# Compression products of a hybrid decoder layer, from full fp32 matmuls to three rounded products each

## What is computed

```
idx = CMP_STRIDE * jnp.arange(n_cmp)[:, None] + jnp.arange(CMP_LEN)[None, :]   # stride 16, length 32
def phi(rows, pe, w1, w2):
    blk = rows[:, idx] + pe[None, None, :, None, :]
    flat = jnp.moveaxis(blk, 3, 2).reshape(b, n_cmp, g, CMP_LEN * hd)
    return jax.nn.silu(flat @ w1) @ w2
kc, vc = rope(phi(k_raw, ...)), phi(v_raw, ...)
```

## Time and profile before

| | us |
|---|---|
| median of 3 runs (985.79 to 986.5) | 986.15 |
| the profiled execution | 986.04 |
| its span, first to last instruction | 984.1 |
| PE busy / DVE / ACT / POOL | 951.6 / 603.8 / 427.8 / 186.7 |

### The profile page before, as it was taken

The page is one execution under the profiler, slowest core; times in us unless marked ns, Lnnn a source line. Parts: engine busy times, 40 slices in busy tenths (PEclk is TensorE's granted clock), DMA queues, the critical chain, the costliest instruction groups (busy, mean ns, idle before and its releaser), DMA issues. The chain is left out here.

```text
span 984.1 us, 21068 instructions
## 1 busy us (share of the span) xinstructions
PE 951.6 (97%) x7852; PEld 865.2 (88%) x7852; DVE 603.8 (61%) x1377; ACT 427.8 (43%) x845; POOL 186.7 (19%) x320
## 2 busy tenths in 40 slices
PE   6999999999998999999999999999999989999996
PEld 6999888998776699999999999899877857999996
DVE  6998666675223467657679976766622225775564
ACT  6444655553220444344444465464521214443343
POOL 1100000337347500000000000003653644000000
PEclk9999999999999999999999999999999989999998
DMA  9673954736669763334546677553675878334421
GB/s 344 237 267 147 394 223 185 289 134 216 213 195 286 235 273 147 138 129 160 198 187 234 274 287 302 214 210 144 215 237 162 250 221 271 159 130 167 175 87 49
DMA packets 65477, 206.30 MB, mean 210 GB/s; under 512 B 12112, under 2 KB 49680, under 8 KB 56032
## 3 DMA queue, kind: packets, MB, share of 16 engines
q1 hardware_dynamic: 56480, 185.31, 51.2%
q0 software_dynamic: 8752, 19.63, 6.6%
q10 hardware_dynamic: 144, 0.01, 0.0%
HBM read 200.12 MB, written 40.18 MB: 244 GB/s over the span
## 5 line engine op out<-in xcount | busy, mean ns | idle before, releaser
L1641 DVE TENSOR_TENSOR big_r<-big,paged_r 128x1024 fp32r<-128x1024 f32 x160 | 195.0, 1223 | 86.5 <-ACT paged_r L1425 84.8
L971 PE MATMUL bank<-xnT_high_r,paged_r 128*128 128x288 f32 x768 | 231.7, 302 | 0.0
L971 PE MATMUL bank<-xnT_r,paged_r 128*128 128x288 f32 x704 | 207.7, 295 | 0.0
L971 PE MATMUL bank<-xnT_high_r,big_r 128*128 128x288 f32 x704 | 207.0, 294 | 0.0
L971 PE MATMUL bank<-short_r,big_r 128*128 128x288 f32 x576 | 170.4, 296 | 0.0
L1425 ACT ACTIVATE paged_r<-big 128x1024 fp32r<-128x1024 f32 x160 | 167.0, 1051 | 6.3 <-DMA big<-in_w_feat 4.0
L971 PEld LDWEIGHTS bank<-xnT_high_r,paged_r 128*128 128x128 f32 x768 | 144.1, 188 | 7.0 <-issue 5.3
L971 PE MATMUL bank<-short_r,paged_r 128*128 128x288 f32 x448 | 134.0, 299 | 9.6 <-DVE big_r L1641 9.4
L971 PE MATMUL bank<-kvp_r,paged_r 128*128 128x288 f32 x448 | 133.4, 298 | 0.0
L971 PEld LDWEIGHTS bank<-xnT_high_r,big_r 128*128 128x128 f32 x704 | 132.5, 188 | 0.0
L971 PEld LDWEIGHTS bank<-xnT_r,paged_r 128*128 128x128 f32 x704 | 132.3, 188 | 0.0
(11 more groups left out here) (317 smaller groups left out, 1466.4 us busy)
## 6 DMA issues: line engine op xcount, KB each, us to landing
big<-in_w_tok SPq DMA_DIRECT2D x13, 2048.0 KB, 8.9
big<-in_w_feat SPq DMA_DIRECT2D x12, 2048.0 KB, 8.4
big<-in_w_gate SPq DMA_DIRECT2D x10, 2048.0 KB, 8.6
out_kept_dil<-in_cache_dil SPq DMA_DIRECT2D x16, 1020.0 KB, 13.6
paged<-in_pool SPq DMA_DIRECT2D x218, 64.0 KB, 2.7
big<-in_w_up SPq DMA_DIRECT2D x12, 1024.0 KB, 9.2
paged<-in_pool POOLq DMA_DIRECT2D x166, 64.0 KB, 2.8
big<-in_kv_win SPq DMA_DIRECT2D x4, 2048.0 KB, 9.3
```

The source lines that it names most:

```text
L971: last = mm(out, l, r, start=(c == 0 and i == 0), stop=(c == n - 1 and i == 2))
L1641: v.tensor_tensor(l_part, full, h_part.bitcast(FP32), ALU.subtract).then_inc(*split_done.inc(s))
```

## The change

Seven things change. (1) A `hid` step is now a piece (hb, kind, bp, lh): one half of the page columns (`bp`), one half of the 8 rows of a column (`lh`), and both parts of w1. It is 4 x 2 x 3 = 24 products of fp32r with 128x128 weights and 256 columns, 16 pieces per layer. (2) ACT rounds the pages of a piece (`pround`, 1024 columns) into one of two buffers, DVE subtracts in place (`psplit`). This is written two pieces ahead: `begin()` stands behind every piece. (3) w1 is rounded and split alike in four quarters per layer (`wround`, `wsplit`), two of them in the units before, two between the first pieces. (4) The rounded w1 of the keys lies in the place of the residual `x`. So `x` is written to HBM by POOL at the start of layer 1 and is loaded again by SP in each layer ahead of the weights of `("gate", 0, 2)`. (5) Pages are loaded, waited for and freed by halves. (6) Both parts of a block now end in one bank after two pieces, and DVE makes one copy, one sum and one product of 256 columns (`hid` with lh = 1), once per `bp`, with a tanh of 256 columns on ACT. (7) `sscore 1 win` moves ahead of the piece 14, and the two `slc` scores of half 0 stand behind it, directly before the last piece (before: behind the 14th step, two steps from the end).

```diff
+    pieces = [(hb, kind, bp, lh) for hb in range(HB) for kind in range(2) for bp in range(2) for lh in range(2)]
+    begun = iter(pieces)
+    begin = lambda: [(kind,) + z for z in itertools.islice(begun, 1) for kind in ("pround", "psplit")]
+    w1_split = lambda kind, part: [("wround", kind, part), ("wsplit", kind, part)]
     blocks = {(0, 1): [("gates",)], (10, 0): [("ghid",)],
               (11, 0): [("ghidt",)], (12, 0): [("gkc",)], (13, 0): [("cscore", 0)], (14, 0): [("cturn", 0)],
-              (14, 1): [("cpv", 0), ("gateC", 0)], (15, 0): [("cscore", 1)]}
+              (12, 1): w1_split(0, 0), (13, 1): w1_split(0, 1),
+              (14, 1): [("cpv", 0), ("gateC", 0)], (15, 0): [("cscore", 1)] + begin(), (15, 1): begin()}
...
-           [("kc", 1)] + part(1, 1, 1, 1) + [("sgateA", 1), ("sscore", 0, "slc0"), ("sscore", 0, "slc1")] + \
-           part(1, 1, 0, 0) + [("sscore", 1, "cmp"), ("sexp", 1, "cmp"), ("sexp", 0, "slc")] + part(1, 1, 0, 1)
-    out += [("sscore", 1, "win"), ("cmpt", 1), ("sturn", 0, "cnew"), ("sscore", 1, "new"), ("sturn", 0, "slc0"), ("imp", 1),
+    done = iter(pieces)
+    piece = lambda: [("hid",) + next(done)] + begin()
+    out += [("sscore", 0, "d4"), ("pv", units[-2])] + piece() + w1_split(1, 0) + \
+           [("sscore", 0, "mix"), ("cturn", 1), ("pturn", units[-1], 0)] + piece() + \
+           [("sexp", 0, "A"), ("cpv", 1), ("pv", units[-1]), ("gateC", 1)] + w1_split(1, 1) + \
+           [("sscore", 0, "win"), ("sscore", 0, "new")] + piece() + \
+           [("sturn", 0, "d4")] + piece() + \
+           [("spv", 0, "d4"), ("sturn", 0, "mix"), ("sexp", 0, "win")] + piece() + \
+           [("spv", 0, "mix"), ("sturn", 0, "anew"), ("kc", 0)] + piece() + \
+           [("spv", 0, "anew"), ("soA", 0)] + piece() + \
+           [("sscore", 0, "cmp"), ("sexp", 0, "cmp"), ("sgateA", 0), ("sscore", 1, "d4")] + piece() + \
+           [("cmpt", 0), ("sscore", 1, "mix"), ("sturn", 0, "win"), ("sexp", 1, "A")] + piece() + \
+           [("vc", 0), ("spv", 0, "win"), ("sturn", 1, "d4")] + piece() + \
+           [("spv", 1, "d4"), ("sturn", 1, "mix"), ("imp", 0)] + piece() + \
+           [("impsum", 0), ("spv", 1, "mix"), ("sturn", 1, "anew")] + piece() + \
+           [("spv", 1, "anew"), ("soA", 1)] + piece() + [("kc", 1)] + piece() + \
+           [("sgateA", 1), ("sscore", 1, "win")] + piece() + \
+           [("sscore", 1, "cmp"), ("sexp", 1, "cmp"), ("sscore", 0, "slc0"), ("sscore", 0, "slc1"), ("sexp", 0, "slc")] + piece()
+    out += [("cmpt", 1), ("sturn", 0, "cnew"), ("sscore", 1, "new"), ("sturn", 0, "slc0"), ("imp", 1),
             ("spv", 0, "cnew"), ("vc", 1), ("sturn", 0, "slc1"), ("sexp", 1, "win"), ("impsum", 1)] + \
            splits(("gate", 0, 0), 0) + \
...
+    x_w, kvp_w = rounded("x", [P, 2048], "_w1"), rounded("kvp", [P, 4608], "_w1")
+    w1_low = rounded("long", [P, 4096], "_w1")
+    W1_HIGH = [[x_w[:, 0:1024], x_w[:, 1024:2048]], [kvp_w[:, 1536:2560], kvp_w[:, 2816:3840]]]
...
+    def page_parts(piece):
+
+        hb, kind, bp, lh = piece
+        slot = PAGE_SLOTS[("cmp", kind, hb)]
+        low = paged_r[slot][:, 2048 * bp:2048 * (bp + 1)].rearrange("p (m l g i) -> p g l m i", m=16, l=8, g=KV)
+        high = page_high[PIECES.index(piece) % 2].rearrange("p (m l g i) -> p g l m i", m=16, l=4, g=KV)
+        return [z.rearrange("p g l m i -> p g m l i") for z in (high, low[:, :, 4 * lh:4 * lh + 4, :, :])]
+
+    def piece_rows(z, piece):
+
+        _, _, bp, lh = piece
+        rows = z[:, 2048 * bp:2048 * (bp + 1)].rearrange("p (m n) -> p m n", m=16)
+        return rows[:, :, 64 * lh:64 * (lh + 1)]
+
+    def piece_high(piece):
+
+        return page_high[PIECES.index(piece) % 2].rearrange("p (m n) -> p m n", m=16)
...
+    def load_pages(queue, key, z, numbers):
+
+        kind, which, hb, h = key
+        if kind == "cmp" and hb == 0:
+            queue.wait_ge(*big_used(Now.layer, split_keys[which - 2]))
+        elif key[0:3] == ("slc", 0, 1):
             queue.wait_ge(*big_used(Now.layer, ("kA", 1)))
-        elif key == ("slc", 1, 1):
-            queue.wait_ge(*pages_used(Now.layer, ("cmp", requests[0] // 2, 1)))
...
         else:
             queue.wait_ge(*pages_used(*PG[z].before(key)))
         for i in page_share(key, z):
             b, g = divmod(i, PAGES)
-            if b in requests:
-                src = a["pool"][Now.layer, bass.ds(numbers[hb][i], 1), :, which + 2 * (kind == "slc"), :]
-                queue.dma_start(pgb(key)[:, b, g, :], src.rearrange("a p n -> (a p) n")).then_inc(*PG[z].fill(key))
...
-                        sp.wait_ge(*pages_used(layer, ("slc", 0, 0)))
-                    elif key == ("up", 0, 0):
-                        load_pages(sp, ("slc", 1, 0), 1, numbers)
-                        load_pages(sp, ("slc", 1, 1), 1, numbers, (2, 3))
+                    at_key = {("vA", 0): both("cmp", 0, 0), ("kA", 1): both("cmp", 1, 0), ("vA", 1): both("cmp", 0, 1),
+                              ("win", 1): both("cmp", 1, 1),
+                              ("gate", 0, 0): both("slc", 0, 1) + both("slc", 0, 0) + [("slc", 1, 1, 0)],
+                              ("up", 0, 0): both("slc", 1, 0) + [("slc", 1, 1, 1)]}
+                    for page_key in at_key.get(key, []):
+                        load_pages(sp, page_key, 1, numbers)
+                    if key == ("gate", 0, 0):
+                        sp.wait_ge(*pages_used(layer, ("slc", 0, 0, 1)))
                     elif key == ("gate", 0, 2):
-                        sp.wait_ge(*pages_used(layer, ("slc", 0, 1)))
+                        sp.wait_ge(*pages_used(layer, ("slc", 0, 1, 1)))
+                        sp.wait_ge(*PJ.is_full(("hid", 1, 0, 1)))
...
+                    pool.wait_ge(*PJ.is_used(("down", 1, 3), 0))
+                    pool.dma_start(x_kept, x[:, :, :]).then_inc(x_stored, 16)
+                elif s == ("rope", "k", 0, 1):
...
-                        last = mm(pj(key)[:, 256 * bp:256 * (bp + 1)], w1[:, kind, 8 * part + l, :],
-                                  pages[:, 16 * bp:16 * (bp + 1), l, :], start=(l == 0), stop=(l == 7))
-                    if bp == 1:
-                        last.then_inc(*PJ.fill(key))
+                    for part in range(2):
+                        pe.wait_ge(*w1_split.at((kind, part)))
+                    pe.wait_ge(*pages_split.at(s[1:]))
+                    ph, pl = page_parts(s[1:])
+                    for j in range(4):
+                        for part in (1, 0):
+                            at = P * (4 * lh + j)
+                            wh = W1_HIGH[kind][part][:, at:at + P]
+                            wl = w1_low[:, 2048 * kind + 1024 * part + at:2048 * kind + 1024 * part + at + P]
+                            out = pj(key)[:, 256 * (1 - part):256 * (2 - part)].rearrange("p (g m i) -> p g m i", g=KV, i=8)
+                            for n, (w, r) in enumerate(((wh, ph), (wh, pl), (wl, ph))):
+                                last = mm(out, w, r[:, :, :, j, :], start=(lh == 0 and j == 0 and part == 1 and n == 0),
+                                          stop=(lh == 1 and j == 3 and n == 2), skip_group_check=True)
+                    last.then_inc(*(PJ.fill(key) if lh else half_done.inc(s[1:])))
                 elif k == "kc":
-                    pe.wait_ge(*hid_done.at(("hid", s[1], 0, 0, 1)))
+                    pe.wait_ge(*hid_done.at(("hid", s[1], 0, 1)))
...
                     f(g_hidt, g_hidp, ACT.Tanh, scale=0.5).then_inc(*hid_tanh.inc(s))
-                elif k == "hid" and s[3:] == (0, 1):
+                elif k == "wround":
+                    kind, part = s[1:]
+                    if kind == 0:
+                        act.wait_ge(*PJ.is_full(("ghid",)))
+                        act.wait_ge(*normed.at(("norm", KT - 1)))
+                        if layer:
+                            act.wait_ge(x_stored, 16)
+                    elif part == 0:
+                        act.wait_ge(*PJ.is_used(("feat", "zb", WT - 1)))
+                    else:
+                        act.wait_ge(*unit_used(UNITS[-1]))
+                    at = 2048 * kind + 1024 * part
+                    f(W1_HIGH[kind][part], long[:, at:at + 1024], ACT.Copy).then_inc(*w1_rounded.inc(s[1:]))
+                elif k == "pround":
+                    n = PIECES.index(s[1:])
+                    hb, kind, bp, lh = s[1:]
+                    for pg in PG:
+                        act.wait_ge(*pg.is_full(("cmp", kind, hb, bp)))
+                    if n == 0:
+                        act.wait_ge(*SC.is_full(("cscore", 1)))
+                    elif n == 1:
+                        act.wait_ge(*PJ.is_used(("feat", "zb", WT - 1)))
+                    else:
+                        before = PIECES[n - 2]
+                        act.wait_ge(*(PJ.is_full(("hid",) + before[0:3]) if before[3] else half_done.at(before)))
```

(33 more changed lines are left out.)

134 lines of the change are left out of this document (49 added, 85 removed).

## The result

The changed kernel takes **979.38 us** (median of 4 runs, 977.87 to 981.17), the kernel before 986.33 us beside it on the same chip (985.79 to 986.53): a ratio of 0.9931, with a 95% interval of 0.9913 to 0.9949. It is faster by 7.0 us. I forecast 967.5 with 957 to 980 as the range, so the direction held, the range held by 0.6 us, and the size did not: 7.0 us of gain where I had 18.6. The profiled execution took 977.87 us, the shortest of the four; its span is 976.2 us at a mean granted clock of 0.997.

What follows compares the result with a forecast made beforehand. PE, busy 97% of the span, was taken to bound the kernel. Layer 0 gives 7.7 us, layer 1 11.5, less 0.3 per layer in the prompt units: 18.6 off 986.04, so 967.5 us; 8 in 10 is 957 to 980.

Steps and rivals of the forecast that it cites:

- The order and the page wait: PE's waits for pages at the slc scores, 2.80 us (layer 0) and 3.81 (layer 1), go, by 1 us of margin.
- The products: Compression products on PE: 120 ns each, a piece 2.96 us against 3.55, giving back 9.4 us per layer.
- the slower rival: Compression products reading runs of 8 at half rate: 227 ns each, about 1040 us, turning at 144 ns; chance 8%.
- Floor: Compression products stay at 133.3 ns because the weights are as wide as before; about 976.5 us; chance 20%.
- w1's pairs in the prompt units: Rounding and subtracting w1 hidden under the projections: 0.3 us per layer, up to 2 x 2.3 if uncovered.
- The waits in the stretch: New PE waits between compression pieces: 3.3 us per layer, including 0.5 at the first output transpose; bounds 0 and 8.
- d4: Transpose of the d4 rows behind piece 2: PE waits 1.6 us for the softmax, where before it had none.
- Banks: Piece 6 needs a bank that DVE frees after piece 5: PE waits 0.9 us.
- The gate weights: First gate product comes 13.3 us after the slc scores at the earliest; PE waits 2.9 us instead of 1.75.
- The spill of x: Storing x and loading it ahead of gate weights: cost 0, up to 6 us per layer if not covered.
- Page rounding and subtraction: Pieces and w1 quarters add 21 us on ACT and 24 us on DVE per layer.
- The signs of being wrong: Pieces of 3.2 us and more; most pieces waiting for DVE's subtraction; a longer prompt stage; a time above 980.

Runs made afterwards that it cites:

- experiment 1: The kernel before with only the order of the score steps changed (window scores earlier, slc scores directly before the last piece); 979.3 us, ratio 0.9939.
- experiment 2: The changed kernel with the four score steps in their old order; 983.59 us, ratio 0.9974.
- experiment 7: The changed kernel with the moving operand read in runs of 16 columns instead of 8 (sums misplaced); 973.03 us in one run.
- experiment 4: The changed kernel with weights of 64 instead of 128 columns in 22 of 24 products of each piece (sums partial); 980.0 us in one run.
- experiment 8: The changed kernel with ACT writing the rounded pages by position, so 16 of 24 products read one run of 256 columns; 972.77 us, ratio 0.9858.
- experiment 3: The changed kernel with the keys' w1 roundings and subtractions placed later in the prompt units and one page pair moved into the stretch; 973.75 us, ratio 0.9884.
- experiment 5: The changed kernel with every compression product on 128 of its 256 columns (sums partial); 1011.52 us in one run.
- experiment 6: The changed kernel with 128 of 256 columns per product and weights of 64 columns in most products (sums partial); 964.9 us in one run.
- 7 to 12: Six variants of the changed kernel: other reading orders, 512-column products, later w1 steps with either reading order, an exponential moved earlier; 968.68 to 976.69 us.

## Why the prediction was right or wrong

- **The order and the page wait: right.** The wait goes in both layers, with the fallen clock; experiment 1 shows it alone, experiment 2 what comes back without it. My margin of 1 us in it held.
- **The products: wrong, and as large as the whole miss.** "I take 120 ns, 106.7 + 13.3" is nearly right for a product that reads runs of 16 or more: 122.3. The kernel reads runs of 8, and pays 133.6. The failed step is that the 13.3 ns were carried over from rows that read whole rows to a kernel that reads runs of 8. A mean piece took 3.35 us instead of 2.96, 12.5 us over 32 pieces. Of these, 8.9 are the run of 8 (the sum of the pieces was 49.1 us per layer in experiment 7, 53.7 and 53.5 here); the rest are the 2 ns above 120 and a start of a piece that takes about 0.14 us and not 0.08. I had the run of 8 in view, as the slower rival, but only as a halving of the rate, with nothing in between; its point of turning, 144 ns, was not reached. Floor's 133.3 ns came true by another mechanism than the one it named (experiment 4), a coincidence, and its 976.5 us is 2.9 away. The rule of the Trainium skill that I weighed there (TensorE: Matmul & The Clock Gate, Wait — 56ns, not 53.3ns?) gives 109 ns for 256 columns, an estimate from its formula; the lowest mean here is 118.2 ns (experiment 8).
- **w1's pairs in the prompt units: wrong.** "I cost them at nothing ... I keep 0.3" was 2.7 us per layer of new waits, and 2.8 us for each layer by experiment 3. The failed step is the cover: the projections hide a pair's own time, but the softmax that stands behind it in DVE's list comes late by it, and PE waits for what follows from that. The text's own bound, up to 2 x 2.3 us, held.
- **The waits in the stretch: the mechanism right, the sizes too high.** d4: 0.87 instead of 1.6, by the chain that I gave (DVE's hidden units, page rounding, maximum, exponential). Banks: 0.3 instead of 0.9. The slower products left DVE more time: with runs of 16 (experiment 7) the d4 wait is 1.16 us, with half of the columns (experiment 5) 1.44, and in each of these kernels the transposes come 4.3 us after the start of the piece before them. The 0.5 us at the first output transpose did not come (0.25, as before). In all this gave back some 1.8 us per layer.
- **The gate weights: direction wrong.** 1.76 us, as before (1.75), not 2.9. A part of it is plain: 13.4 us passed from the slc scores' end (324.29) to the gate product (337.67), my 13.3, but the last piece was 0.35 longer, and behind it PE now waits 0.94 us for the copy into PTc, 0.2 before; I had no term for that, and experiment 1 has it too.
- **The spill of x: not contradicted.** No wait names it. It was not tried alone.
- **Page rounding and subtraction, 21 and 24 us per layer: right**, 38 and 49 us in all.
- **The signs of being wrong.** Of the four that I named, two came: pieces of 3.2 us and more, and a prompt stage that is longer than before.

In sum, against the profiled execution (977.87, so 10.4 us over the forecast): +12.5 for the pieces, -4.8 for the waits at d4, banks and gate (0.7, 0.6 and 1.1 per layer), -1.0 for the output transposes, +1.4 for PTc, +4.7 for the prompt units, +1.0 in the first projection, which experiment 1 has too, -0.8 in the tail, and some -2.6 of small terms that I have not placed. The pieces save 6.7 us (57.0 to 53.7 per layer) where I had 18.9, and the new waits in the prompt units (5.4) and at d4 (1.7) eat it: so experiment 1 and the changed kernel come out equal.

## What to carry to other kernels

When an operation is replaced by one that the trace shows only on whole rows, ask for its pace in the reading order that it will have: here another walk over the same numbers, runs of 16 for runs of 8, was worth 6 us (experiment 7, one run), and one copy that had to be made anyway could write the better order for nothing (experiment 8). When steps are put into the lists of helper engines that are half idle, look for what stands behind them in the list at that place, not at the engine's share: two pairs of 2.3 us took 2.7 us of PE in each layer, and moved by a few steps they took 0.7. And try a change of order alone before a larger rewrite that contains it.

## What the runs showed of the hardware

- fp32r products with 128x128 weights, at the whole clock, start 133.3 ns apart on 256 columns in runs of 8 (133.6 in the piece shown), 121.7 in runs of 16 (122.3), 236 on 512 columns in runs of 32, 111 on 128 columns; with 64 columns of weights and 128 moving, 60 in the rows shown and 64 on average. Why runs of 8 cost 11 ns is open, and so is how much of it is the length of the run and how much the third dimension of the walk.
- That price is not fixed for each product: with the 8 of 24 that read runs of 8 among unbroken ones, the mean is 122.9 ns (experiment 8).
- Products paced by their weight loads start 111 ns apart at the whole clock and 213 ns apart at the granted clock of 0.50 (experiment 5).
- In experiment 5, with half the columns per product at nearly the same distance, the clock was at 1.2 GHz for 110 us in all, and the kernel lost 25 us against the kernel before. With half the weights' columns too (experiment 6), at 64 ns, the mean clock was 0.98. Each is one run. Less work in each product is not less time if the clock falls with it.
- In most of the other kernels here (experiments 2, 4 and 7 to 12) the clock was at 0.50 for stretches of 3.5 or 7 us that the changed kernel's profile does not have, each behind a wait of PE: in experiment 8 behind the 1.76 us at 231.01 and the 0.94 us at 800.53. The changed kernel's profile has the same two waits with no fall behind them; but its other executions had a mean clock of 0.991 to 0.996 where the profiled one had 0.997. This is part of the spread of 2 to 7 us, and limits how finely these kernels can be compared.
